# A hybrid decoder layer: pooling tables loaded among the weights, another order of the first tiles, a tail in three pieces, decode loads reckoned longer

## The reference

```
hn = rms_norm(h, norm_w);  proj = hn @ w_in          # 1024 -> 6144
u, gp, q, k, v, gr = split(proj, 1024 each)
pool:  trailing means over 2/4/8/16 rows (4 groups of channels) minus u,
       then per group a 256x256 map (w_pool) times pool_scale, times silu(gp)
ret:   rotary q, k; per chunk of 128:  scores = q k^T * decay mask
       o = scores v + decayed q S;  S = g^128 S + decayed k^T v   # 8 heads, S 128x128
       o = rms_norm per head * ret_norm_w * silu(gr)
h = h + concat(pool, ret) @ w_out;  y = rms_norm(h, final_norm_w)
decode: the same with L = 1, S and the last 15 rows of u from the inputs
outputs: y of prompt and decode, S and pooling rows of both
```

## Time and profile before

| | us |
|---|---|
| median of 3 runs | 607.85 |
| lowest and highest run | 602.15, 611.97 |
| profiled execution | 605.21 |
| its span on the slowest core (5) | 603.7 |
| spans of the 8 cores | 592.9 to 603.7 |
| PE busy on that core | 559.6 (93%) |
| DVE, ACT, POOL busy | 402.1, 291.2, 105.1 |

### The profile page before, as it was taken

One profiled execution on the slowest core, in us unless ns is written; L12 is line 12 of the kernel. 1 busy time (PEld: TensorE's weight loads), 2 busy tenths in 40 slices (PEclk: granted clock), 3 DMA queues, 4 the chain that ended last, 5 costly groups with the idle time before them and its releaser, 6 DMA issues.

```text
span 603.7 us, 14127 instructions; the slowest of 8 cores (592.9 to 603.7 us)
## 1 busy us (share of the span) xinstructions
PE 559.6 (93%) x4524; PEld 317.6 (53%) x4524; DVE 402.1 (67%) x1058; ACT 291.2 (48%) x864; POOL 105.1 (17%) x130
## 2 busy tenths in 40 slices
PE   0889999699999999999999999988999999899994
PEld 0434455586545556555555546454464654446671
DVE  2369786847877677746766776847777572865565
ACT  2347678348954435443535354533545444435331
POOL 3410010111010201010101132221412221322010
PEclk9899999799999999999999999989999999899998
DMA  8999999368354344524233376656765865649203
GB/s 161 192 189 168 171 186 214 72 96 158 87 123 129 94 104 110 140 71 110 88 64 117 77 210 126 161 147 123 204 143 160 172 125 137 124 109 184 44 1 109
DMA packets 76547, 78.53 MB, mean 130 GB/s; under 512 B 55534, under 2 KB 59262, under 8 KB 74412
## 3 DMA queue, kind: packets, MB, share of 16 engines
q1 hardware_dynamic: 73020, 57.94, 39.1%
q0 software_dynamic: 3456, 19.70, 18.9%
HBM read 64.34 MB, written 18.41 MB: 137 GB/s over the span
## 4 chain that ended last, share of the span: by engine, by line
PE 79%; DMA 13%; DVE 3%; issue 2%; ACT 1%; POOL 1%; SPq 1%; DVEq 0%; POOLq 0%; ACTq 0%
PE pp L586 40%; PE pp L891 17%; PE pp L602 9%; DMA scr<-S_in 7%; DMA w_in_bf<-w_in 4%; PE pp L837 2%; DMA xA<-meta 2%; PE pp L945 1%; PE pp L818 1%; PE pp L707 1%; PE pp L724 1%; PE pp L748 1%; PE pp L750 1%; DMA y<-xr 1%; PE pp L552 1%
## 5 line engine op out<-in xcount | busy, mean ns | idle before, releaser
L586 PE MATMUL pp<-w_in_bf,hnTs 128*128 128x512 bf16 x1120 | 261.1, 384 | 8.0 <-DVE hnTs L573 5.3
L586 PEld LDWEIGHTS pp<-w_in_bf,hnTs 128*128 128x128 bf16 x1120 | 105.7, 99 | 129.5 <-issue 19.3
L891 PE MATMUL pp<-w_out_bf,yT 128*128 128x512 bf16 x448 | 100.7, 379 | 0.3
L623 ACT ACTIVATE F<-pp,pack 128x128 f32<-128x128 f32 (+1 forms) x216 | 61.6, 371 | 56.9 <-PE pp L586 42.2
L522 POOL TENSOR_TENSOR sm<-sm,nh 128x4 f32<-128x4 f32 (+2 forms) x49 | 44.0, 898 | 246.5 <-DVE sm L519 245.2
L891 PEld LDWEIGHTS pp<-w_out_bf,yT 128*128 128x128 bf16 x448 | 42.8, 98 | 51.6 <-issue 2.3
L939 POOL TENSOR_TENSOR scr<-vM,pack 16x512 bf16<-16x512 bf16 x32 | 34.8, 1087 | 133.8 <-PE pp L945 116.5
L900 ACT ACTIVATE pp<-xr 128x512 f32<-128x512 f32 x30 | 18.1, 603 | 79.1 <-DVE xr L898 61.6
L602 PE MATMUL pp<-hnTs,w_in_bf 128*128 128x128 bf16 x896 | 54.7, 222 | 0.0
L602 PEld LDWEIGHTS pp<-hnTs,w_in_bf 128*128 128x128 bf16 x896 | 52.5, 100 | 1.9 <-issue 0.2
L786 DVE SCALAR_TENSOR_TENSOR ry<-pp,sm,G 128x128 bf16<-128x128 f32 x104 | 29.1, 343 | 21.6 <-POOL sm L522 21.4
(11 more groups left out here) (176 smaller groups left out, 736.4 us busy)
## 6 DMA issues: line engine op xcount, KB each, us to landing
w_in_bf<-w_in POOLq DMA_DIRECT2D x12, 1024.0 KB, 35.5
scr<-S_in SPq DMA_DIRECT2D x32, 256.0 KB, 4.5
Ss<-scr SPq DMA_DIRECT2D x32, 256.0 KB, 3.4
xr<-x SPq DMA_DIRECT2D x15, 512.0 KB, 4.0
y<-xr SPq DMA_DIRECT2D x15, 512.0 KB, 3.3
xA<-x SPq DMA_DIRECT2D x12, 512.0 KB, 3.9
w_out_bf<-w_out POOLq DMA_DIRECT2D x4, 1024.0 KB, 13.8
w_out_bf<-x POOLq DMA_DIRECT2D x2, 512.0 KB, 17.5
```

Of the source, the lines that this page charges most:

```text
L586: r = e.matmul(bk(b)[:T, :], lhsT=h.ap[:, kc * T:(kc + 1) * T], rhs=w_in_bf[:, c0 // 512, kc, :], start=(kc == 0), stop=(kc == 7))
L623: r = e.activation(out=Fa.ap[:T, i * 128:(i + 1) * 128], in_=bk(b)[:T, i * 128:(i + 1) * 128], func=AF.Copy, scale=dec[:T, dslot * 8 + h:d ...
L891: r = e.matmul(bk(b)[:T, :], lhsT=yap[:, kc * 128:kc * 128 + T], rhs=w_out_bf[:, kc, nt * 512:(nt + 1) * 512], start=(kc == 0), stop=(kc = ...
```

## The change

Five edits. (1) The pooling tables are loaded by POOL in queue "w", after block 9 and ahead of block 4. (2) Order0 is 1, 2, 0, 3, 4; x of tile 2 is loaded ahead of all weights, block 10 in two halves (and its products for tiles 0 to 4 in two groups of four kc), and x of tiles 3 and 4 stand further ahead: tile 4's goes to yT, no longer to xA. (3) The loads of blocks 11 and 6 and what stands behind them are told to come behind the powers of tiles 1, 2 and 0 (`behind`), the squares of tile 2 come behind those of tile 1, and tile 0's mean comes behind the eviction of tile 1; tile 1's eviction is split, five chunks on DVE and three on ACT. (4) The last tile's `outp` works in pieces of 512, 256 and 256 columns; the product with finw is taken ahead of the power, into scr, and the two halves are scaled by DVE and ACT and stored by SP and by ACT. (5) `pad=3.0` for the decode loads is added to the planner's rank and to the time at which what reads them may start; the nominal cost of a POOL issue goes from 0.9 to 0.6. What runs is the same but for the pieces; what changes besides is the whole planned order.

```diff
         for t in reversed(tasks):
-            t.rank = t.cost + t.bias + max([self.lag(t, s) + s.rank for s in t.suc] + [s.rank for s in t.qsuc] + [0.0])
+            t.rank = t.cost + t.bias + max([self.lag(t, s) + t.pad + s.rank for s in t.suc] + [s.rank for s in t.qsuc] + [0.0])
...
+                lagv += t.pad
                 est[n] = max(est[n], t.end + lagv)
...
-                    cost=0.9 if eng == "pool" else 0.5, size=nbytes, bias=bias, queue=queue)
+                    cost=0.6 if eng == "pool" else 0.5, size=nbytes, bias=bias, queue=queue, pad=pad)
...
-    def load_w(blk):
-        dma("pool", w_in_bf[:, blk, :, :].rearrange("p a b -> p (a b)"), w_in[blk], [], wk(blk), 1 << 21, queue="w")
+    def load_w(blk, half=None, behind=()):
+        k0, k1 = (0, 8) if half is None else (4 * half, 4 * half + 4)
+        dma("pool", w_in_bf[:, blk, k0:k1, :].rearrange("p a b -> p (a b)"), w_in[blk, :, k0 * 512:k1 * 512], behind,
+            wk(blk, half), (k1 - k0) << 18, queue="w")
...
-        rstd(ss_x, rs_x, c, 1, 0, T, 1.0 / D, "ss_x%d" % c, "rs_x%d" % c)
+        rstd(ss_x, rs_x, c, 1, 0, T, 1.0 / D, "ss_x%d" % c, "rs_x%d" % c, None, () if t else hnT[1].k[:1])
...
-        b = tr_mm(T, hb)
+        n = 5 if t == 1 else 8
+        b = tr_mm(T, hb, 0, n)
...
+            P.op("act", ev2, reads=[b2, "normw"], writes=d.k[1:], cost=c_act(8 - n, T, ptr=1))
...
-        for nt in range(2):
+        chunks = [(0, 512), (512, 256), (768, 256)] if fin else [(0, 512), (512, 512)]
+        z = scf(0, 4)
+        for n, (c0, w) in enumerate(chunks):
...
+            if fin:
+                P.op("dve", lambda e, sl=sl: e.tensor_tensor(out=z.ap[:, sl], in0=xb.ap[:, sl], in1=finw_b[:, sl],
+                                                             op=ALU.mult),
...
+        P.op("dve", lambda e: e.tensor_scalar(out=z.ap[:, 0:512], in0=z.ap[:, 0:512], scalar1=rs_f[:, 0:1], scalar2=None,
+                                              op0=ALU.mult), reads=z.k[0:4] + ["rs_f"], writes=z.k[0:4], cost=0.5)
+        P.op("act", lambda e: e.activation(out=z.ap[:, 512:1024], in_=z.ap[:, 512:1024], func=AF.Copy, scale=rs_f[:, 0:1]),
+             reads=z.k[4:8] + ["rs_f"], writes=z.k[4:8], cost=c_act(1, 512, ptr=1))
+        for i, eng in enumerate(("sp", "act")):
+            sl = slice(512 * i, 512 * i + 512)
+            dma(eng, y[(NT - 1) * 128:, sl], z.ap[:, sl], z.k[4 * i:4 * i + 4], [], 1 << 18, "d_y%d" % i)
...
-            Sinb[s % 3].k, 1 << 18, "d_sl%d" % (s % 3))
+            Sinb[s % 3].k, 1 << 18, "d_sl%d" % (s % 3), pad=3.0)
...
-    order0 = (1, 0, 2, 3, 4)
-    load_w(WORD[0])
+    order0 = (1, 2, 0, 3, 4)
     load_x(2, stage[2], "w")
+    load_w(WORD[0], 0)
+    load_w(WORD[0], 1)
     load_cs(1, "w")
     load_cs(0, "w")
-    load_w(WORD[1])
     load_x(3, stage[3], "w")
-    load_cs(2, "w")
-    load_w(WORD[2])
     for i, t in enumerate(order0):
-        if t == 4:
-            load_x(4, xA, "w")
+        if t == 0:
+            load_w(WORD[1], None, ["rs_x1"])
+            load_cs(2, "w", ["rs_x2"])
+        if t == 3:
+            load_x(4, stage[4], "w", ["rs_x0"])
+            load_w(WORD[2])
...
     for i in range(4, 10):
         load_w(WORD[i])
+        if i == 5:
+            dma("pool", yT_t[:].bitcast(F32), pool_scale[0:1, :].broadcast_to([128, D]), [], yTk, 1 << 19, queue="w")
+            dma("pool", scr[:, :].bitcast(F32).rearrange("p (g cc d) -> p g cc d", g=4, cc=2),
+                w_pool.rearrange("g (cc p) d -> p g cc d", p=128), [], sc(0, 8).k, 1 << 20, queue="w")
...
-    dma("sp", scr[:, :].bitcast(F32).rearrange("p (g cc d) -> p g cc d", g=4, cc=2),
-        w_pool.rearrange("g (cc p) d -> p g cc d", p=128), ["win0"], sc(0, 8).k, 1 << 20, queue="late")
-    dma("sp", yT_t[:].bitcast(F32), pool_scale[0:1, :].broadcast_to([128, D]), ["win0"], yTk, 1 << 19, queue="late")
```

More of the change, by code:

```diff
@@ L471, in build_program, with dma @@
     uniq = [0]
[L473 removed]
+    def dma(eng, out, in_, reads, writes, nbytes, sem=None, bias=0.0, queue=None, pad=0.0):
         if sem is None:
@@ L550, in tr @@
             r = None
-            for c in range(8):
+            for c in range(c0, c1):
                 r = e.transpose(out=bkb(b)[:, c * T:(c + 1) * T], in_=src.ap[:T, c * 128:(c + 1) * 128],
@@ L575, in ev, with ev2 @@
             return r
-        P.op("dve", ev, reads=[b, "normw"], writes=d.k, cost=c_dve(8, T))
+        P.op("dve", ev, reads=[b, "normw"], writes=d.k[:1] if n < 8 else d.k, cost=c_dve(n, T))
+        if n < 8:
+            b2 = tr_mm(T, hb, n, 8)
+            def ev2(e):
+                r = None
+                for kc in range(n, 8):
+                    r = e.activation(out=d.ap[:, kc * T:(kc + 1) * T], in_=bkb(b2)[:, kc * T:(kc + 1) * T],
+                                     func=AF.Copy, scale=normw[:, kc:kc + 1])
+                return r
+            P.op("act", ev2, reads=[b2, "normw"], writes=d.k[1:], cost=c_act(8 - n, T, ptr=1))
     def pj_mm(t, c0):
@@ L581, in pj_mm, with mm @@
         b = Bank()
-        def mm(e):
-            r = None
-            for kc in range(8):
-                r = e.matmul(bk(b)[:T, :], lhsT=h.ap[:, kc * T:(kc + 1) * T],
-                             rhs=w_in_bf[:, c0 // 512, kc, :], start=(kc == 0), stop=(kc == 7))
-            return r
-        P.op("pe", mm, reads=h.k + wk(c0 // 512), writes=[b], cost=c_pe(8, 512))
+        blk = c0 // 512
+        for half in ((0, 1) if blk == WORD[0] and t <= NG else (None,)):
+            def mm(e, half=half):
+                r = None
+                for kc in range(4 * (half or 0), 4 if half == 0 else 8):
+                    r = e.matmul(bk(b)[:T, :], lhsT=h.ap[:, kc * T:(kc + 1) * T],
+                                 rhs=w_in_bf[:, blk, kc, :], start=(kc == 0), stop=(kc == 7))
+                return r
+            P.op("pe", mm, reads=h.k + wk(blk, half) + ([b] if half else []), writes=[b],
+                 cost=c_pe(8 if half is None else 4, 512))
         return b
@@ L907, in outp @@
-        P.op("dve", lambda e: e.scalar_tensor_tensor(
-            out=rs_f[:T, :], in0=ss_f[:T, 1:2], scalar=1.0 / D, in1=ss_f[:T, 2:3], op0=ALU.mult, op1=ALU.add),
-            reads=["ss_f1", "ss_f2"], writes=["rs_f"], cost=0.17)
+                        r = e.matmul(bk(b)[:T, 0:w], lhsT=yap[:, kc * 128:kc * 128 + T],
+                                     rhs=w_out_bf[:, kc, sl], start=(kc == 0), stop=(kc == 15))
+                    return r
+                P.op("pe", mm, reads=yk[4 * half:4 * half + 4] + WOK[16 * half:16 * half + 16] + ([b] if half else hk),
+                     writes=[b], cost=c_pe(8, w))
```

95 lines of the change are left out of this document (49 added, 46 removed).

## The result

The changed kernel takes 597.63 us (median of 4 runs, 595.32 to 598.46), the kernel before 606.76 beside it (602.15 to 611.97): a ratio of 0.9867, interval 0.9832 to 0.9902. It is 8 to 9 us faster, where 18 were forecast. (Executions that stood far above the others of their kernel are left out of the figures here.) The profiled execution took 598.46 us.

A forecast was written before the change was run, and what follows sets the result against it. The prediction took PE to be full except for long waits at the start, the first pooling matmuls and the decode states, plus slow clock behind pauses. Savings of 18.2 us from 607.85 gave 590 us, range 580 to 601.

The forecast's parts named there:

- Decode loads: From 380 to 540 us: reckoning loads 3 us longer removes PE's S_in waits; 7 us saved, bounds 11 and none.
- Rival 1: Decode waits for S_in stay because the planner's clock is nominal; 11.2 us saved in all, 597 us; chance 0.18.
- The weights behind the tables: Block 4 and later blocks come 4.7 us later by bytes, at 63.9 us; PE asks at 65.9, so no cost.
- rival 3: Tables take 38.6 us in the weights' queue; PE stands 31.9 us for block 4; 624 us; chance 0.05.
- the 2 us to spare: Margin between block 4's forecast landing at 63.9 us and PE asking for it at 65.9.
- The table multiply: DVE's multiply making w_pool_bf, 2.29 us, moves into 41 to 100 us, where 7.7 us free on DVE cover it.
- Pooling tables, 7.0 saved: At the first pooling matmuls: 5.0 us pause and 2.8 of slow clock go, 0.8 kept back; bounds 8.3 and 3.
- the 0.8 kept for the attention chains: Held back from 7.8 us because DVE's attention chains of tiles 2 and 3, hidden in the pooling pause, come late next.
- The start, 3.3 saved: Before 41 us: ten groups instead of eight stand ahead of block 7, giving PE more work; bounds 3.8 saved, 1 lost.
- The tail: From last add to last scaling: smaller pieces, scaling side by side; 0.9 us saved, 3.3 left; bounds 1.6 saved, 0.5 lost.
- The sum: Savings at start, pooling, weights, decode and tail: 3.3 + 7.0 + 0 + 7.0 + 0.9 = 18.2 us.
- Rival 2: DVE becomes the bound early, held by the table multiply; up to 6.3 of 7.0 us come back; 596; chance 0.10.

The follow-up runs named there:

- b_pad: The kernel before with the decode loads reckoned 3 us longer and nothing else; 599.11 us, ratio 0.9860.
- b_tab: The kernel before with the two pooling tables in the weights' queue ahead of block 4 and nothing else; 600.37 us, ratio 0.9887.
- a_cost9: The changed kernel with the planner's price of an issue on POOL back at 0.9 us, nothing else; 594.44 us, ratio 0.9771.
- c_old9: The kernel before with tables in the weights' queue, decode loads reckoned 3 us longer and the new tail; old start, POOL issue at 0.9; 595.39 us, ratio 0.9781.
- a_oldstart: The changed kernel with the start of before (order, block 10 in one piece, x loads, no forced order); 597.37 us, ratio 0.9830.

## Why three terms of the prediction held and the start and the sum did not

- **Decode loads: right.** 7.8 us of lost time went against 7 forecast, and no wait for S_in is left. 1.3 came back from 160 to 380, where the steps now stand (1.7 in b_pad, which has the padding alone). Rival 1 did not happen; that its time, 597, is the nearest to the measured 597.63 is luck.
- **The weights behind the tables: covered, but at a higher price than 4.7 us.** In the changed kernel PE waits for no block after 17 us, so rival 3 fell. On core 1 block 9 was issued at 17.7 and block 4 at 32.2 us:

```profile
w_in_bf<-w_in POOLq DMA_DIRECT2D x1, 1024.0 KB, 35.3
w_in_bf<-w_in POOLq DMA_DIRECT2D x1, 1024.0 KB, 35.2
```

  Block 9 of before was issued at 19.6 on core 5:

```profile
w_in_bf<-w_in POOLq DMA_DIRECT2D x1, 1024.0 KB, 33.4
```

  So block 9 landed at 53.0 both times, and block 4 at 67.3 instead of 59.2: 8.1 us later, not 4.7. From block 9's landing to w_pool's it is 7.8 us in the mean of the cores (6.9 in b_tab). That is far less than 38.6 us, which fits the Trainium skill's rule of turns between queues (DMA: Bandwidth & Descriptors, section Queues, rings and completion order), but it is more than the bytes, and the 2 us to spare do not hold it: in b_tab PE stands for this block on four cores (0.6 to 2.0 us), in a_cost9 on three (0.5 to 1.9). Why 7.8 and not 4.7 stays open.
- **The table multiply: right.** It has no idle time before it, as against the 5.74 us of the earlier trace rows:

```profile
61.85 2.29 DVE L1101 TENSOR_TENSOR w_pool_bf<-scr,yT 128x2048 bf16<-128x2048 f32 x1
```

- **Pooling tables, 7.0 saved: right alone.** b_tab saves 6.7 us, and the 0.8 kept for the attention chains behind the pause is what it loses more than before from 120 to 160 (2.2 against 1.4). In the changed kernel 100 to 120 gained 4.2 in the mean, and the same stretch's slow clock went; but 120 to 160 lost 4.3 more. On core 1 that is 2.1 us at 123.3, 2.0 at 153.0 and two pieces of 3.4 us at half clock behind them (the clock lists 0.50 there), 7.5 in all. Share by stretch, with the clock in the third column from the end:

```profile
123.30:126.70 3.40, 3.37 (x8) 1.13 (x8) 0.13 (x1) 1.93 (x4) 0.00 (x0) 0.50 1.14 167
154.00:157.40 3.40, 3.40 (x25) 2.17 (x23) 3.02 (x9) 3.05 (x20) 1.40 (x1) 0.50 1.10 207
```

  The second wait is the fold's, shown above; cores 1, 3, 4 and 6 have it, and three of these are the slowest. It came with the tables, since b_tab has it too. With the old start this stretch loses only 2.3 (c_old9), so most of the 4.3 is the start's gain handed back, at the first wait above all.
- **The start, 3.3 saved: the step that failed.** "What counts is how much work PE has by the time block 7 is there" took a gain ahead of block 7 for a gain at the end, and the sum gave the price of an issue on POOL no term. The size by 41 was right for another order: with 0.9 us as the price the start loses 3.1 less than before (a_cost9), inside the bounds; in the changed kernel 1.0. The price chose the order in which PE stands for tile 3. That costs 0.8 to 2.1 by 41 in three pairs of executions, 2.4 in the mean of the cores, and 3 to 4 us of the time (3.2 and 4.2 in the two comparisons). And of either start nothing is left at 160: the changed kernel has lost 31.6 and a_oldstart 30.6, a_cost9 30.7 and c_old9 30.6.

  Where it goes, PE's rows show: first core 1 of the changed kernel, then core 3 of c_old9 and core 1 of a_cost9.

```profile
121.07 0.10 PEld L603 LDWEIGHTS pp<-w_in_bf,xr 128*128 128x128 bf16 x1
123.33 1.01 PE L603 MATMUL pp<-w_in_bf,xr 128*128 128x512 bf16 x2 [2.10 <-issue]
```

```profile
121.74 0.38 PE L603 MATMUL pp<-w_in_bf,xr 128*128 128x512 bf16 x1 [1.07 <-issue]
```

```profile
120.71 0.17 PE L838 MATMUL pp<-pack,us 128*128 128x16 bf16 x1 [2.12 <-issue]
```

  The weights are loaded and the matmul does not come, at the first of a group, at the last, and in the middle, with no semaphore between. What these places have in common is their number: each time it is the 1724th or 1725th of PE's instructions (loads of weights, matmuls and waits counted), on every core and in every kernel where PE stands here, before included. A load of 16 KB in the queue that the profile names "instruction" ends 1.1 to 1.7 us before PE goes on; on core 1 of the changed kernel it is one packet:

```profile
q8 instruction: 1, 0.02, 1.0%
```

  So PE waits for its own instructions here, not for DVE. (On cores 2 and 4 of the changed kernel the profile does name DVE, but their records lack 61 matmuls.) Means of the six cores with all records, in us:

| | PE comes to this instruction | stands | goes on |
|---|---|---|---|
| c_old9 (old start) | 122.1 | 0.7 | 122.8 |
| a_oldstart (old start) | 122.0 | 0.3 | 122.2 |
| changed kernel | 121.2 | 2.3 | 123.5 |
| a_cost9 (new start) | 120.6 | 2.0 | 122.7 |

  PE comes 1 us earlier and goes on no earlier, and behind the longer stand the clock falls on some cores. The prediction looked for lateness in the blocks of w_in and asked of nothing else whether it moves with PE. As time, the new start is worth 1.0 us between a_cost9 and c_old9 (594.44 and 595.39; 1.5 in the mean of the cores), less than the intervals can tell, and nothing in the changed kernel (a_oldstart). c_old9, with old start and old price, is faster than the changed kernel: its ratio of 0.9781 reaches up to 0.9819, that of the changed kernel (0.9867) down to 0.9832.
- **The tail: 0.9 forecast, 0.6 measured,** on core 1 from 588.96 to 592.62, 3.66 us against 4.23, and the same on every core. ACT's store took 2.5 us and SP's 2.1, so ACT as an issuer costs 0.4.

```profile
588.96 0.42 DVE L919 TENSOR_TENSOR xA<-xA,pp 128x256 f32<-128x256 f32 x1 [0.43 <-PE pp L914]
...
591.25 0.56 POOL L937 TENSOR_TENSOR sm<-sm,nh 128x1 f32<-128x1 f32 x1 [7.23 <-DVE sm L929]
591.90 0.72 ACT L948 ACTIVATE scr<-scr,sm 128x512 f32<-128x512 f32 x1 [1.80 <-POOL sm L937]
591.91 0.49 DVE L946 TENSOR_SCALAR scr<-scr,sm 128x512 f32<-128x512 f32 x1 [0.87 <-POOL sm L937]
```

- **The sum.** Tables, padding and tail measured together give 12.4 us (11.0 to 15.7) instead of 14.9; the start adds 1.0 instead of 3.3; the price takes 3.2 to 4.2: 9.2 to 10.2 by medians of separate comparisons, 8 to 9 measured directly. So start and price together took 2.2 to 3.2 where 3.3 were to be saved, and that is most of what is missing from 18.2. The terms of tables and padding were read on the slowest core of one execution and held for the slowest core; in the mean of the cores they are 1.3 to 1.7 smaller. Rival 2 did not happen: DVE was not held up by the multiply, though it is busy 18.8 of 20 us from 100 to 120.

What stays open: what sets the time of that load of instructions (no run changed their number or when they are fetched), why the tables take 7.8 us in the queue, and which release pins the progress at 160 beside the two waits.

## What to carry to other kernels

Before terms are added, ask for each where the engine that gains time meets the next thing that does not move with it (here PE's own instructions, and loads of w_out in front of the masks): a gain ahead of that point can be handed back there, whatever its size. In a kernel whose order a planner makes, a changed price is a change of order; give it a term, and look at which ready work stands behind a wait in the first rows. Where the profile names no releaser, count the engine's instructions up to the wait and look at the instruction queue. Judge parts by the mean of the cores, and the whole by the slowest.
